# A decoder layer on one core: the seam between the output projection and the gated feed-forward is reordered, and the matmul operands on both sides of it get one address modulo 512 bytes

## The reference, cut to what matters

```python
def reference(x, ...):
    ...
    mixed = jnp.concatenate([y_mla, y_dn], axis=-1)      # attention heads beside DeltaNet heads
    h = h + mixed @ w_out[l]                             # output projection, 1024 x 1024
    h = h + _conv_glu(_rmsnorm(h, ffn_norm_w[l]), w_gate[l], w_up[l], ffn_conv_w[l],
                      ffn_conv_b[l], w_down[l])
    return h[:, N_META:]

def _conv_glu(h, w_gate, w_up, ffn_conv_w, ffn_conv_b, w_down):
    gate = _causal_dwconv(h @ w_gate, ffn_conv_w) + ffn_conv_b
    return (jax.nn.silu(gate) * (h @ w_up)) @ w_down
```

## The kernel before

| buffer | role | modulo 512 |
|---|---|---|
| w_ring | stationary in gate-up, both in down | 256 |
| us_hi and us_lo of U_2 to U_5, us_hi6, us_lo0 | moving in gate-up | 256 |
| us_hi0 | moving in gate-up, stationary in down | 192 |
| us_hi1, us_lo1 | moving | 416 |
| us_lo6 | moving in gate-up | 128 |
| wo_m0, wo_m1 (m_hi, m_lo of even and of odd tiles) | stationary in output | 128, 192 |
| w_out split: ot_rows; do_k_lo, do_v | moving in output | 256; 416, 416 |
| at_v of heads 0 and 2 (do_v) against at_pt | stationary, moving in attention | 416, 256 |

## Time and profile before

### The profile page before, as it was taken

One profiled execution on the slowest core, in us unless ns is written; L12 is line 12 of the kernel. 1 busy time (PEld: TensorE's weight loads), 2 busy tenths in 40 slices (PEclk: granted clock), 3 DMA queues, 4 the chain that ended last, 5 costly groups with the idle time before them and its releaser, 6 DMA issues.

```text
span 2947.3 us, 50196 instructions
## 1 busy us (share of the span) xinstructions
PE 2791.2 (95%) x19675; PEld 2418.9 (82%) x19675; DVE 1815.8 (62%) x2759; ACT 1186.9 (40%) x2210; POOL 1140.7 (39%) x1213
## 2 busy tenths in 40 slices
PE   7998979997999899997998899999899999999999
PEld 7997779997888788886887688888788888788887
DVE  3225934444555777777796777766977776543544
ACT  3225722224555455554443433333433333331321
POOL 2534940004788000003553565666666665100000
PEclk9999989998999899999999999999999999999999
DMA  8975953225463123222576433333533333654554
GB/s 269 353 253 166 275 179 112 69 76 133 115 158 81 41 67 101 67 67 90 186 254 220 143 94 97 93 108 98 177 113 94 102 108 117 224 183 135 186 171 140
DMA packets 403282, 421.14 MB, mean 143 GB/s; under 512 B 34075, under 2 KB 325995, under 8 KB 401000
## 3 DMA queue, kind: packets, MB, share of 16 engines
q1 hardware_dynamic: 368400, 298.61, 33.7%
q10 hardware_dynamic: 19944, 66.63, 6.9%
q0 software_dynamic: 14704, 52.69, 5.4%
HBM read 257.51 MB, written 160.34 MB: 142 GB/s over the span
## 4 chain that ended last, share of the span: by engine, by line
PE 48%; DVE 3%; DMA 1%; ACT 0%; issue 0%; POOL 0%; POOLq 0%; SPq 0%; ACTq 0%; DVEq 0%
PE ot_p L3658 28%; PE ot_p L3021 14%; PE ot_p L2759 5%; DVE fu_us_lo L3462 1%; DMA fu_us_lo<-scr_u2T 1%; PE ot_p L2774 0%; PE ot_p L2745 0%; PE ot_p L3670 0%; DMA fu_w_raw<-in_w_down 0%; DMA fu_w_raw<-in_w_gate 0%; DMA scr_tT<-ot_t_more 0%; DVE fu_acc L3540 0%; DMA fu_b_third<-in_w_down 0%; DVE fu_w_ring L3469 0%; ACT fu_us_hi L3331 0%
## 5 line engine op out<-in xcount | busy, mean ns | idle before, releaser
L3658 PE MATMUL ot_p<-fu_us_hi,fu_w_ring 128*128 128x512 f32 x2464 | 778.0, 395 | 17.5 <-DVE fu_us_lo L3462 17.1
L3658 PEld LDWEIGHTS ot_p<-fu_us_hi,fu_w_ring 128*128 128x128 f32 x2464 | 466.6, 189 | 129.6 <-DVE fu_us_lo L3462 20.4
L3658 PE MATMUL ot_p<-fu_us_lo,fu_w_ring 128*128 128x512 f32 x1232 | 487.0, 395 | 0.0
L3658 PEld LDWEIGHTS ot_p<-fu_us_lo,fu_w_ring 128*128 128x128 f32 x1232 | 233.3, 189 | 49.8
L3021 PE MATMUL ot_p<-fu_us_hi,fu_w_ring 128*128 128x512 f32 x666 | 169.9, 392 | 1.9 <-DVE fu_w_ring L2944 1.9
L3469 DVE TENSOR_TENSOR fu_w_ring<-fu_w_raw,fu_w_ring 128x512 fp32r<-128x512 f32 x88 | 108.2, 1229 | 97.3 <-ACT fu_w_ring L3342 97.3
L3286 POOL TENSOR_TENSOR fu_w_ring<-fu_w_raw,fu_w_ring 128x512 fp32r<-128x512 f32 x44 | 60.6, 1377 | 244.0 <-ACT fu_w_ring L3342 244.0
L3342 ACT ACTIVATE fu_w_ring<-fu_w_raw 128x512 fp32r<-128x512 f32 x132 | 83.1, 629 | 177.5 <-PE ot_p L3658 174.8
L3514 DVE SCALAR_TENSOR_TENSOR fu_acc<-fu_gb,fu_taps,fu_acc 128x1024 f32<-128x1024 f32 x88 | 130.2, 1481 | 39.0 <-ACT fu_acc L3389 38.2
L2944 DVE TENSOR_TENSOR fu_w_ring<-fu_w_ring 128x1408 fp32r<-128x1408 f32 x37 | 60.8, 1643 | 146.1 <-ACT fu_w_ring L2893 146.1
L2078 ACT ACTIVATE at_pt_hi<-at_pT 128x512 fp32r<-128x512 f32 (+3 forms) x176 | 92.6, 539 | 143.2 <-PE at_pT L2343 142.3
(11 more groups left out here) (552 smaller groups left out, 7151.5 us busy)
## 6 DMA issues: line engine op xcount, KB each, us to landing
fu_w_ring<-scr_gs ACTq DMA_DIRECT2D x37, 704.0 KB, 4.5
fu_w_raw<-in_w_gate SPq DMA_DIRECT2D x22, 1024.0 KB, 5.3
fu_w_raw<-in_w_up SPq DMA_DIRECT2D x22, 1024.0 KB, 5.2
scr_gs<-fu_sg SPq DMA_DIRECT2D x84, 256.0 KB, 3.2
scr_gs<-fu_acc SPq DMA_DIRECT2D x63, 256.0 KB, 2.8
fu_us_lo<-scr_gs ACTq DMA_DIRECT2D x19, 704.0 KB, 4.5
pj_wd<-in_w_down POOLq DMA_DIRECT2D x11, 1024.0 KB, 9.4
scr_td<-pj_td POOLq DMA_DIRECT2D x11, 1024.0 KB, 6.4
```

The costliest lines, as they stand in the source:

```text
L3658: p = pe.matmul(bank(2 * n + m, i)[:, :], a[:, k, :], x[:, k, :], start=(k == 0 and n_pass == 0), stop=(k == HALVES_K - 1 and n_pass == 2))
```

## The change

It has three parts.

1. **Queues at the seam.** SyncE: store_joined(12) goes ahead of the wait for `cleared`; store_joined(14) goes from behind U_1's load to behind the up weights' load (`load_w(0, 1)`); before U_5's load stands a new wait for join(14) (`t_step` 32). ScalarE: u_part(14) before the first weight split; the weight split of U_5 ahead of U_2's token copy and that of U_6 ahead of U_4's, instead of in the loop. VectorE: `taps_out` right behind norm2_dve(15) instead of in the loop behind join(15); join(14) behind U_0's low part instead of ahead of it; norm2_dve(16) ahead of U_2's weight split, and the splits of U_3 and U_4 one step later; join(15) behind U_6's low part instead of ahead of it. TensorE: turn2(14) behind a wait for `cleared`, then the turn of the taps (now into bank 1) and then multiply(16); the first halo_products behind U_5 instead of U_4, waiting for u_part(16) instead of the taps.
2. **The left block.** wo_m0 and wo_m1 become one block of 2L floats. Attention uses the same places as before; the output projection's m_hi and m_lo and gate-up's us_lo6 and us_hi0 begin 32 floats further and follow each other without the 64 bytes between them.
3. **The right room.** A room of 40 floats (160 bytes) is set at the right end. It holds two small tiles of the attention stage, and all that lies left of it moves by 160 bytes: do_k_lo, do_v, the attention's q_lo and rope tiles, us_hi1 and us_lo1.

By the sizes, after the change us_hi0, us_lo6, us_hi1, us_lo1, m_hi, m_lo, do_k_lo and do_v all begin at 256 modulo 512, as w_ring and ot_rows do.

```diff
@@ -37,6 +37,7 @@
 OUT_EARLY, OUT_SPLIT = 4, 3
+REST_ROW, M_SKIP = 40, 32
 OUT_STEPS = ("eps_set", "z_exp", "z_one", "squared", "summed", "log", "rooted", "gated", "yg_ready", "mixed", "turned", "m_half",
@@ -1912,7 +1913,8 @@
         ez, yg, mix = (ez0, ez1), S["wo_raw"][:, 0, :], S["wo_raw"][:, 1, :]
-        out_st, eps = r.sb("out_st", [P, 3, 2 * HEADS]), r.sb("eps", [P, 1])
+        NST = 3 * 2 * HEADS
+        out_st, eps = S["at_rest"][:, 0:NST].rearrange("p (x h) -> p x h", x=3), S["at_rest"][:, NST:NST + 1]
         step = S["wo_step"]
@@ -2415,7 +2417,7 @@
 
-    m, raw = S["wo_m"], S["wo_raw"]
+    m, raw = [S["wo_block"][:, M_SKIP + 2 * D * i:M_SKIP + 2 * D * (i + 1)] for i in range(2)], S["wo_raw"]
     z = [f(m[1][:, 0:DNW]), f(m[1][:, DNW + D:2 * DNW + D])]
@@ -2424,7 +2426,7 @@
 OutParts = collections.namedtuple("OutParts", """sync gpsimd scalar vector tensor store_joined store hi u_part norm2_act lo join
-    norm2_dve normed turn2 multiply banks turned multiplied h2_ready xn_ready
+    norm2_dve normed turn2 multiply banks turned m_ready multiplied h2_ready xn_ready
     xn_turned u_out h2_stored u_stored t_step t_stored rows_free cleared""")
@@ -2779,10 +2781,10 @@
         span(0, TILES, TILES, (0, lambda t, s, u: turn(t, s, u) if t >= 2 else None),
-             (-1, lambda t, s, u: multiply(pe, t) if t else None), (-2, lambda t, s, u: turn2(pe, t)))
+             (-1, lambda t, s, u: multiply(pe, t) if t else None), (-2, lambda t, s, u: turn2(pe, t) if t < TILES - 3 else None))
 
     return OutParts(sync, gpsimd, scalar, vector, tensor, store_joined, store, hi, u_part, norm2_act, lo, join, norm2_dve, normed,
-                    turn2, multiply, banks, turned, multiplied, h2_ready, xn_ready,
+                    turn2, multiply, banks, turned, m_ready, multiplied, h2_ready, xn_ready,
                     xn_turned, u_out, h2_stored, u_stored, t_step, t_stored, rows_free, cleared)
@@ -3040,6 +3042,7 @@
     AHEAD = RING - 1
+    TAPS_BANK = 1
     BANKS = 8
@@ -3047,7 +3050,8 @@
     taps_both = r.sb("taps", [P, 2, P])
-    us_lo6, us_hi0 = (r.sb(x, [P, L], F32R)[:, 0:UNIT].rearrange("p (k n) -> p k n", n=B) for x in ("us_lo6", "us_hi0"))
+    m_block = r.sb("m_block", [P, 2 * L], F32R)[:, M_SKIP:M_SKIP + 2 * UNIT]
+    us_lo6, us_hi0 = (m_block[:, i * UNIT:i * UNIT + UNIT].rearrange("p (k n) -> p k n", n=B) for i in range(2))
     sw_late, b_third = r.sb("sw_late", [P, 2, HALVES_K, P]), r.sb("b_third", [P, B])
@@ -3061,6 +3065,7 @@
     r.sb("out_small", [P, 72])
+    right.sb("rest", [P, REST_ROW])
     us_hi1 = right.sb("us_hi1", [P, L], F32R)[:, 0:UNIT].rearrange("p (k n) -> p k n", n=B)
@@ -3193,10 +3198,10 @@
 
+        out.store_joined(sp, 12)
         sp.wait_ge(out.cleared, 1)
...
             sp.wait_ge(out.u_stored[i], 16 * n)
-        out.store_joined(sp, 12)
         for x in out.t_stored:
@@ -3204,7 +3209,6 @@
         load_u(0, 1)
-        out.store_joined(sp, 14)
         sp.wait_ge(out.rows_free, 5)
@@ -3212,6 +3216,7 @@
         load_u(0, 3)
+        sp.wait_ge(out.t_step, 4 * 8)
         sp.wait_ge(out.u_stored[1], 16 * 3)
@@ -3220,6 +3225,7 @@
         load_w(0, 1)
+        out.store_joined(sp, 14)
         out.store_joined(sp, 15)
@@ -3403,18 +3409,19 @@
         out.norm2_act(act, 15)
+        out.u_part(act, 14)
         split(0)
-        out.u_part(act, 14)
         u_part(0, 0)
...
         u_part(0, 1)
-        for i in range(2, AHEAD):
+        for i in range(2, RING):
             split(i)
...
         u_part(0, 3)
+        split(RING)
         u_part(0, 4)
@@ -3427,7 +3434,7 @@
                     u_part(0, 6)
-                if q + AHEAD < UNITS_7 * PHASES:
+                if RING < q + AHEAD < UNITS_7 * PHASES:
                     split(q + AHEAD)
@@ -3452,7 +3459,7 @@
             dve.wait_ge(taps_turned, 1)
-            dve.tensor_copy(taps[:, :], pM[BANKS - 1][:, 0:(TAPS + 1) * FT]).then_inc(taps_ready, 1)
+            dve.tensor_copy(taps[:, :], pM[TAPS_BANK][:, 0:(TAPS + 1) * FT]).then_inc(taps_ready, 1)
             dve.wait_ge(id_made, 2)
@@ -3547,19 +3554,20 @@
         out.norm2_dve(dve, 15)
+        taps_out()
         out.normed(dve, 15)
         split(0)
+        u_part(0, 0)
         out.join(dve, 14)
-        u_part(0, 0)
         split(1)
         u_part(0, 1)
+        out.norm2_dve(dve, 16)
         split(2)
-        out.norm2_dve(dve, 16)
-        split(3)
         u_part(0, 2)
         out.normed(dve, 16)
+        split(3)
+        u_part(0, 3)
         split(4)
-        u_part(0, 3)
         for ph in range(PHASES):
@@ -3568,8 +3576,7 @@
                     u_part(0, 6)
-                if ph == 0 and i == 4:
-                    taps_out()
+                    out.join(dve, 15)
                 if q + AHEAD < UNITS_7 * PHASES:
@@ -3580,8 +3587,6 @@
                         make_u2(ph)
-                        if ph == 0:
-                            out.join(dve, 15)
                     if i == 3:
@@ -3625,18 +3630,18 @@
             pe.wait_ge(consts, 32)
-            pe.wait_ge(out.u_out[0], 9)
-            pe.transpose(pM[BANKS - 1][:, 0:n_taps], taps_in[:, :], ident[0:n_taps, 0:n_taps]).then_inc(taps_turned, 1)
+            pe.wait_ge(out.m_ready[0], 8)
+            pe.transpose(pM[TAPS_BANK][:, 0:n_taps], taps_in[:, :], ident[0:n_taps, 0:n_taps]).then_inc(taps_turned, 1)
 
         def bank_free(q):
+            if q == TAPS_BANK:
+                pe.wait_ge(taps_ready, 1)
             if q in (2, 3):
...
                 pe.wait_ge(out.h2_ready[0], 9)
-            if q == 6:
+            if q in (6, 7):
                 pe.wait_ge(out.u_out[0], 9)
-            if q == BANKS - 1:
-                pe.wait_ge(taps_ready, 1)
             if q < BANKS:
@@ -3661,7 +3666,7 @@
             if n == 0:
-                pe.wait_ge(taps_ready, 1)
+                pe.wait_ge(out.u_out[0], 9)
                 pe.wait_ge(head_loaded, 16)
@@ -3680,8 +3685,10 @@
 
+        pe.wait_ge(out.cleared, 1)
+        out.turn2(pe, 14)
+        turn_taps()
         out.multiply(pe, 16)
-        pe.wait_ge(out.cleared, 1)
         out.turn2(pe, 15)
@@ -3689,9 +3696,7 @@
                         out.turn2(pe, 16)
-                    if n == 0 and m == 0 and i == 3:
-                        turn_taps()
-                    if m == 0 and i == (1 if n else 4) and halo_set(n):
+                    if m == 0 and i == (1 if n else 5) and halo_set(n):
                         halo_products(n)
@@ -3785,7 +3790,7 @@
         r = Room(nc, delta_to_out, "do", "right")
-        S["at_k_lo"], S["at_v"] = r.sb("k_lo", [P, L], F32R), r.sb("v", [P, SEQ // P, 2, VD], F32R)
+        S["at_rest"], S["at_k_lo"], S["at_v"] = r.sb("rest", [P, REST_ROW]), r.sb("k_lo", [P, L], F32R), r.sb("v", [P, SEQ // P, 2, VD], F32R)
         r = of_delta = Room(nc, delta_to_attention, "da", "right")
@@ -3797,7 +3802,8 @@
         S["wo_loaded"], S["wo_gains"] = r.sems("loaded", KD), r.sem("gains")
-        S["wo_m"] = [r.sb(f"m{i}", [P, L], F32R) for i in range(2)]
+        S["wo_block"] = r.sb("m", [P, 2 * L], F32R)
+        S["wo_m"] = [S["wo_block"][:, i * L:i * L + L] for i in range(2)]
         S["wo_y1"], S["wo_o_sb"], S["wo_stored"] = r.sb("y1", [P, 2 * HEADS, P]), r.sb("o_sb", [P, AT_QB, VD]), r.sem("stored")
```

## The result

The changed kernel takes **2919.5 us**, the median of four runs (2917.07 to 2920.74), against 2946.39 us for the kernel before, timed on the same chip: a ratio of 0.9903, with a 95% interval of 0.9886 to 0.9921, or 27 us less. It is faster by more than the 0.2% that can be told, but the forecast of 2902.5 is 17 us too low, and 2919.5 lies above the range's end of 2916.

What follows compares the result with a forecast made beforehand. TensorE, busy for 95% of the span, was taken as the bound, with gains from its idle seam and its pace: 22.5 + 10.0 + 6.5 + 4.0 + 1.0 = 44.0 us less, median 2902.5 us, 8-in-10 range 2894 to 2916.

Steps and rivals of the forecast that it cites:

- The seam: Between output and gate-up's second phase: reordered loads and joins start the up phase at 1630, not 1652.67, gaining 22.5 us.
- `cleared` never held turn2(14): In the seam, turn2(14)'s new wait for `cleared` was costed at nothing, with 4.7 us of slack.
- Term (e): In the seam, VectorE's work behind the up weights (1621), join(15) at 2.8 to 7 us, puts the up phase at 1630.
- Is anything else later than that?: Seam check: VectorE's other work, 24 us from 1596, ends by 1620, TensorE's by 1624, so neither is later.
- The prediction's own sign of being wrong: At the seam: forecast wrong if the up phase starts more than 35 us after the output's last transposes.
- Rival 2: At the seam, up weights become the new wait, landing at 1629.7; seam gives 11.5 us, total 2913.5; chance 0.13.
- Gate-up's pace: In gate-up's 44 phases, equal addresses bring every unit to 2.72 us, 0.24 us a phase: 10.0 us gained.
- Output's pace: In the output projection, each of 17 tiles falls from 11.27 to 10.88 us: 6.5 us gained.
- Down: In the down projection, which reads the same buffers, 2.2 ns for each of 1848 matmuls: 4.0 us gained.
- Attention: In attention, do_v moves to its partner's address, speeding 168 matmuls: 1.0 us gained, bounds -1 and +3.
- The range: For the whole kernel, 8 in 10: 2894 to 2916 us, taking in rival 2 and a us or two for the run.
- half an effect of the address: Case within the range, for the whole kernel: the address helps half as much, 33 us less, 2913.

Runs made afterwards that it cites:

- joins_narrow: The changed kernel with join(15) and join(16) cut to 8 of each 512 columns, the rest of those sums left out: 2909.8 us, ratio 0.9866.
- pool_narrow: The changed kernel with GpSimd's eight weight sums of phases 1 and 2 cut to 4 of 128 columns, VectorE's instructions untouched: 2908.6 us, one run.
- pad_only: The kernel before with the layout edits alone, its queues unchanged: 2935.5 us, ratio 0.9954.
- queues_only: The changed kernel with the old layout, so only the queues at the seam are reordered: 2931.8 us, ratio 0.9939.
- residues: A separate kernel of 33 runs of 24 float32r matmuls with shifted operand starts: 226.7 ns per matmul at difference 0, up to 240.0 at 68.
- before_again: The kernel before, unchanged, run once more for a second profile: 2947.2 us.

## Why the prediction was wrong in size

**The seam, 22.5 against 13.7: the step that failed.** Its first half held. The output's end moved up by 4.7 us, where some 6 were forecast. With 4.7 taken off, the first weights' load was due at 1580.3 and went out at 1580.3, and the up weights were due at 1616.3 and had landed by 1616.8; of the two waits of the earlier trace rows the taps' went, while 5.0 of the 9.2 us for low parts stayed; `cleared` never held turn2(14), which starts at 1584.15, right at its tile's end. Term (e) then summed VectorE's instructions behind the up weights, with "2.8 to 7" for join(15) as GpSimd is quiet or not, and took about the middle. Measured were 1.78 for the split and 4.8 for join(15). The first half of the seam came to 32.1 us, where the forecast's 1630 less 1600.7 makes 29.3: 2.8 us short.

The larger part, some 6 us, came from the paragraph "Is anything else later than that?". It added VectorE's work up to 1620 at quiet durations, compared it with the start of phase 1 and stopped there. VectorE was in fact busy for 29.8 of the 33 us from 1596 to 1629, and began phase 1 with the results of phase 0's last units and join(16) still to do: join(16) began 6.0 us after phase 1 did (1634.10 against 1628.15), where it had begun 1.5 us ahead of it before. The debt fell due where TensorE next waits long for VectorE, at the halo products of phase 2, which made the phase 6.3 us longer: 5.0 of waiting, and the rest of it TensorE's slower work behind the wait (last section). `joins_narrow` and `pool_narrow` bear out the two halves of this cause, VectorE's own work and its slowing; in the latter the seam gives 21.6 of the 22.5. The prediction's own sign of being wrong, a phase 1 more than 35 us behind the output's last transposes, would not have caught this: it came 30.9 behind them. The sign looked, like the sum, no further than the start of phase 1.

**Rival 2** had the right engine and a figure near the result, 2913.5, by another way: it put the delay on up weights that land at 1629.7. They landed at 1616.8. It is wrong as a mechanism.

**Gate-up's pace, 10.0 against 10.2: right mechanism, and the close number is partly luck.** Of the 10.2, 31 plain phases at 0.23 us and 9 with halo products at 0.15 make 8.5, and `pad_only`, with 8.2, shows the cause. The other 1.6 are phase 22, where the second half's operands are loaded (31.7 before, 30.1 after), for which nothing was forecast. They don't come from the address: the phase takes 31.7 in `pad_only` and 30.1 in `queues_only`. It takes 31.9 in `joins_narrow`, though, with the queues of the change, so what makes them is open.

**Output's pace, 6.5 against 4.1: right mechanism, wrong size.** The sum took four times U_3's 2.72 as the tile's floor. The tile takes 10.98 at the padded address, 0.10 us above 48 times 226.7 ns, and the 11.27 of before must have held the same 0.10; so 0.29 us are saved and not 0.39, and 17 of them are 4.8. (By the table of `residues` it should be less still; the odd tiles of before were slower than their addresses say.) The rest is within what this stretch varies by: 220.9, 221.2, 221.3, 221.4 and 222.7 to 222.9 in profiles with the same layout.

**Down, 4.0 against 1.9.** The items themselves gave 2.9 us (400.4 to 397.5 from the fourth item to the last matmul; 397.4 in `pad_only`; 401.4 in `queues_only`, 401.0 in `before_again`), for 53 of the 56 items, to which the term gives 3.8. The pace is what was forecast: items of 7.48 to 7.60 us became 7.48 each. But 1.0 us goes to a new wait of one item for VectorE's split of w_ring (2746.2). Down's first three items took 1.0 us longer, in `queues_only` 2.3 and in `before_again` 0.7 longer. That is the same kind of wait, two of them, 4.9 us before and 6.0 after, 6.4 in `queues_only` and 5.8 in `before_again`. As it grows without any change too, its cause stays open.

**Attention, 1.0: not there in the rows that it was made from.** The start of output varies by 8 us between profiles, so its 0.6 in the table means nothing. The matmuls of do_v themselves can be read. From start to start, the 112 with the high part took 251.6 ns in the mean before and 250.6 after, the 56 with the low part 232.9 and 233.9: 0.1 us in all. They run in threes, fewer than the 5 to 11 matmuls of settling, which would account for it. The scores were not looked at.

**The range** took the seam's end from rival 2 and half an effect of the address. It held no case in which a gain at the first wait is given back at a later one.

## What to carry to other kernels

When a wait is removed, add up the work of the engine that it waited for, at contended durations, not up to the next wait but until that engine has a slack again: what it owes is presented at the first later place that needs it, here 20 us on. An operation of VectorE with both inputs in SBUF can cost over 1 us more beside GpSimd's, even if it has 8 elements, so the moment at which GpSimd works can matter more than who does what. Where float32r matmuls of 512 columns run back to back in long series, start both operands at one address modulo 256 bytes; for other shapes nothing here was measured.

## What was not expected of the hardware

- The pace of matmuls that follow each other without a gap goes with the difference of the two operands' addresses modulo 256 bytes: 226.7 ns at 0 and up to 240.0 at 68, 5.9% more. The sign counts (64: 228.9, 192: 233.3), and a misalignment of 4 bytes (234.4) is worse than one of 128 (231.7).
- After an interruption the pace needs 5 to 11 matmuls to settle at equal addresses. At others it can keep what came before: 233.3 or 228.9 ns at the same two addresses.
- An operation of VectorE over 8 elements took 1.25 us beside GpSimd's sums, and 0.16 without them.
- The 16 halo matmuls took 1.93 us behind the 5.0 us in which TensorE stood idle, at a granted clock of 0.50 (1657.90 to 1659.80), the 1.2 GHz level, and 1.07 in `pool_narrow`, at 1.00. Phase 2 is 6.5 us longer than the steady 20.76, of which the wait is 5.0: it costs another 1.5 us, 0.9 of them in these 16. In `joins_narrow`, behind a wait of 1.0, they took 1.07.
